# A two-layer encoder with a product-key expert stage: the next layer's inputs loaded in thirteen pieces beside thirteen tiles of the second table

## What is computed

```python
q = (xt @ w_query).reshape(T, PEER_HEADS, 2, PEER_DK // 2)
s = jnp.einsum('thpd,phkd->thpk', q, sub_keys)
s_top, i_top = lax.top_k(s, PEER_TOPK)
...
ue = jnp.take(u_tab, ib, axis=0)
a = jax.nn.gelu(jnp.einsum('thkd,td->thk', ue, xb), approximate=False)
ve = jnp.take(v_tab, ib, axis=0)
return jnp.einsum('thk,thkd->td', (gb * a).astype(ve.dtype), ve)
```

## Time and profile before

| | |
|---|---|
| median of three runs | 2057.51 us (2055.43 to 2057.92) |
| profiled execution, its own time | 2052.14 us |
| its span in the trace | 2050.3 us |
| PE busy in the span | 1958.4 us (96%) |
| granted clock of TensorE, mean | 0.988 of full speed |
| PE's share of the chain that ended last | 88% |
| DMA's share of that chain | 1% |
| second table's stage, layer 0 and layer 1 | 664 to 1023 us, 1680 to 2040 us |

### The profile page before, as it was taken

The page is one execution under the profiler, slowest core; times in us unless marked ns, Lnnn a source line. Parts: engine busy times, 40 slices in busy tenths (PEclk is TensorE's granted clock), DMA queues, the critical chain, the costliest instruction groups (busy, mean ns, idle before and its releaser), DMA issues.

```text
span 2050.3 us, 43061 instructions
## 1 busy us (share of the span) xinstructions
PE 1958.4 (96%) x12792; PEld 1786.3 (87%) x12792; DVE 1320.7 (64%) x2869; ACT 1103.0 (54%) x2124; POOL 770.4 (38%) x553
## 2 busy tenths in 40 slices
PE   7989998999999999999998999989999999999997
PEld 6779997999999887888777799979999998878886
DVE  4655699666666665666546557986666666656665
ACT  4344454666665554555533454546666555555554
POOL 4433599576770000000054316995777600000000
PEclk9999999999999999999999999999999999999999
DMA  5215454444344556555522154544343455565555
GB/s 209 74 42 174 153 178 144 153 143 140 137 142 173 187 194 235 192 194 194 185 73 82 55 182 150 179 145 151 134 143 135 141 178 191 194 244 194 194 190 179
DMA packets 90470, 327.05 MB, mean 160 GB/s; under 512 B 10400, under 2 KB 11168, under 8 KB 89760
## 3 DMA queue, kind: packets, MB, share of 16 engines
q1 hardware_dynamic: 90400, 326.18, 46.0%
HBM read 325.09 MB, written 1.05 MB: 159 GB/s over the span
## 4 chain that ended last, share of the span: by engine, by line
PE 88%; DVE 5%; issue 3%; POOL 2%; DMA 1%; ACT 1%; SPq 1%; DVEq 0%; POOLq 0%; ACTq 0%
PE ps L795 12%; PE ps L796 12%; PE ps L797 12%; PE ps L868 11%; PE ps L871 11%; PE ps L870 11%; PE ps L814 6%; PE ps L768 2%; PE ps L771 1%; PE ps L770 1%; POOL tab_lo L1239 1%; DVE work L1345 1%; DMA raw<-tab_v 1%; PE ps L579 1%; PE ps L545 1%
## 5 line engine op out<-in xcount | busy, mean ns | idle before, releaser
L1239 POOL TENSOR_TENSOR tab_lo<-raw,tab_hi 128x512 fp32r<-128x512 f32 x416 | 586.3, 1425 | 262.0 <-ACT tab_hi L1071 181.2
L795 PE MATMUL ps<-x_lo,tab_hi 128*128 128x256 f32 x2048 | 591.8, 289 | 22.1 <-POOL tab_lo L1239 18.9
L797 PE MATMUL ps<-x_hi,tab_lo 128*128 128x256 f32 x2048 | 579.1, 283 | 0.0
L796 PE MATMUL ps<-x_hi,tab_hi 128*128 128x256 f32 x2048 | 579.0, 283 | 0.0
L1652 DVE TENSOR_TENSOR tab_lo<-raw,tab_hi 128x512 fp32r<-128x512 f32 x512 | 354.2, 692 | 280.0 <-ACT tab_hi L1166 276.2
L1071 ACT ACTIVATE tab_hi<-raw 128x512 fp32r<-128x512 f32 x504 | 317.5, 631 | 338.9 <-PE ps L797 334.4
L795 PEld LDWEIGHTS ps<-x_lo,tab_hi 128*128 128x128 f32 x2048 | 392.0, 191 | 25.7 <-POOL tab_lo L1239 25.4
L868 PE MATMUL ps<-tab_lo,w_hi 128*128 128x512 f32 x1024 | 400.6, 391 | 7.5 <-DVE w_lo L1660 7.5
L870 PE MATMUL ps<-tab_hi,w_hi 128*128 128x512 f32 x1024 | 399.8, 390 | 0.0
L871 PE MATMUL ps<-tab_hi,w_lo 128*128 128x512 f32 x1024 | 399.8, 390 | 0.0
L796 PEld LDWEIGHTS ps<-x_hi,tab_hi 128*128 128x128 f32 x2048 | 392.5, 192 | 0.0
(11 more groups left out here) (204 smaller groups left out, 2527.5 us busy)
## 6 DMA issues: line engine op xcount, KB each, us to landing
raw<-tab_u SPq DMA_DIRECT2D x256, 512.0 KB, 3.2
raw<-tab_v SPq DMA_DIRECT2D x256, 512.0 KB, 3.2
raw<-w_proj SPq DMA_DIRECT2D x68, 512.0 KB, 3.5
raw<-w_proj SPq DMA_DIRECT2D x16, 384.0 KB, 3.1
work<-cdft SPq DMA_DIRECT2D x3, 1536.0 KB, 9.5
work<-cfilter SPq DMA_DIRECT2D x3, 768.0 KB, 5.4
work<-sub_keys SPq DMA_DIRECT2D x2, 1024.0 KB, 5.5
work<-pmat SPq DMA_DIRECT2D x3, 352.0 KB, 6.2
```

What stands on the lines that cost most here:

```text
L795: mm(bank, hi, x_lo[:, 4 * h + k, :], start=(h + k == 0), stop=False)
L796: mm(bank, hi, x_hi[:, 4 * h + k, :], start=False, stop=False)
L797: last = mm(bank, lo, x_hi[:, 4 * h + k, :], start=False, stop=(h + k == 4))
L1239: tt(half(tab_lo, s, h), half(raw, s, h), half(tab_hi, s, h).bitcast(F32), ALU.subtract).then_inc(lo_pool.sem, 1)
```

## The change

The eight DMAs between tiles 47 and 48 of the second table are gone. The same data is loaded in fifteen DMAs in thirteen steps, one step behind the issue of each of the tiles 36 to 48. Step 0 has the two filter inputs and `pvec`, steps 1 and 2 the rest of `pmat` in two pieces of 608 columns, steps 3 to 5 the rest of `cfilter` in three of 512, steps 6 to 11 `cdft` in six of 512, and step 12 `gain_qk`. The two waits on the split weights now stand behind the issue of tile 36. Tiles 36 to 51 are written out instead of looped. The start of the program makes its loads with the same helpers, so there too 5 DMAs become 12.

```diff
+PARAM_MATS, PARAM_PIECES, DFT_PIECES = 2, 5, 6
+FOLLOWING = 1 + PARAM_PIECES + DFT_PIECES + 1
...
-        params_in = sig("params_in", 48)
-        dft_in = sig("dft_in", 16)
+        params_in = sig("params_in", 16 * PARAM_PIECES)
+        dft_in = sig("dft_in", 16 * DFT_PIECES)
...
-            def load_params(layer):
-                sp.dma_start(fm[:, 192:704], pmat[layer, :, 192:704]).then_inc(params_in.sem, 16)
-                sp.dma_start(fc[:, 256:CF_N], cfilter[:, 256:CF_N]).then_inc(params_in.sem, 16)
-                sp.dma_start(fm[:, 704:1408], pmat[layer, :, 704:1408]).then_inc(params_in.sem, 16)
-
-            def load_late_params(layer):
-                sp.dma_start(dft, cdft[:, :]).then_inc(dft_in.sem, 16)
-                sp.dma_start(gqk, gain_qk[layer, :, :]).then_inc(gqk_in.sem, 16)
+            def load_params(layer, piece):
+
+                if piece < PARAM_MATS:
+                    a, b = 192 + 608 * piece, 192 + 608 * (piece + 1)
+                    sp.dma_start(fm[:, a:b], pmat[layer, :, a:b]).then_inc(params_in.sem, 16)
+                else:
+                    a, b = 256 + 512 * (piece - PARAM_MATS), 256 + 512 * (piece - PARAM_MATS + 1)
+                    sp.dma_start(fc[:, a:b], cfilter[:, a:b]).then_inc(params_in.sem, 16)
+
+            def load_late_params(layer, piece):
+                if piece < DFT_PIECES:
+                    a, b = 512 * piece, 512 * (piece + 1)
+                    sp.dma_start(dft[:, a:b], cdft[:, a:b]).then_inc(dft_in.sem, 16)
+                else:
+                    sp.dma_start(gqk, gain_qk[layer, :, :]).then_inc(gqk_in.sem, 16)
+
+            def load_following(layer, piece):
+
+                if piece == 0:
+                    load_filter_inputs(layer)
+                    sp.dma_start(pv[:, :], pvec[layer, :, :]).then_inc(pv_in.sem, 16)
+                elif piece <= PARAM_PIECES:
+                    load_params(layer, piece - 1)
+                else:
+                    load_late_params(layer, piece - 1 - PARAM_PIECES)
...
-                with sp.Fori(0, 12) as i:
+                with sp.Fori(0, 9) as i:
                     stream(i, tab_v, lo_dve, LO_V)
 
 
-                sp.wait_ge(*at(whi_done, l, LOADED_AHEAD // SEQ + 1))
-                sp.wait_ge(*at(wlo_done, l, LOADED_AHEAD // SEQ + 1))
-                load_filter_inputs(following)
-                load_params(following)
-                load_late_params(following)
-                sp.dma_start(pv[:, :], pvec[following, :, :]).then_inc(pv_in.sem, 16)
-                with sp.Fori(12, 32) as i:
+                for j in range(36, 52):
+                    load_tile(j, tab_v, lo_dve, LO_V)
+                    if j == 36:
+                        sp.wait_ge(*at(whi_done, l, LOADED_AHEAD // SEQ + 1))
+                        sp.wait_ge(*at(wlo_done, l, LOADED_AHEAD // SEQ + 1))
+                    if j - 36 < FOLLOWING:
+                        load_following(following, j - 36)
+                with sp.Fori(13, 32) as i:
                     stream(i, tab_v, lo_dve, LO_V)
...
-                pe.wait_ge(*at(params_in, l, 48))
+                pe.wait_ge(*at(params_in, l, 16 * PARAM_PIECES))
```

More of the change, by code:

```diff
@@ L377, in _ @@
             load_channels(0, 1)
-            load_params(0)
+            for piece in range(PARAM_PIECES):
+                load_params(0, piece)
             load_channels(0, 2)
             load_channels(0, 3)
-            load_late_params(0)
+            for piece in range(DFT_PIECES + 1):
+                load_late_params(0, piece)
             with sp.Fori(0, DEPTH) as l:
@@ L411, in _, with load_tile @@
                     sp.dma_start(raw[:, n, :], tab_u[l, n, :, :]).then_inc(raw_in[n].sem, 16)
+                def load_tile(j, table, signal, offset, s=None):
+                    slot = j % 4 if s is None else s
+                    sp.wait_ge(*at(signal, l, j * 2 + offset - 6))
+                    sp.dma_start(raw[:, slot, :], table[l, j, :, :]).then_inc(raw_in[slot].sem, 16)
                 def stream(i, table, signal, offset):
                     for s in range(4):
-                        j = i * 4 + s
-                        sp.wait_ge(*at(signal, l, j * 2 + offset - 6))
-                        sp.dma_start(raw[:, s, :], table[l, j, :, :]).then_inc(raw_in[s].sem, 16)
+                        load_tile(i * 4 + s, table, signal, offset, s)
                 with sp.Fori(1, EARLY // 4 + 1) as i:
@@ L449, in _ @@
             sp.wait_ge(mlp_in.sem, (DEPTH + 1) * 32)
-            sp.wait_ge(params_in.sem, (DEPTH + 1) * 48)
-            sp.wait_ge(dft_in.sem, (DEPTH + 1) * 16)
+            sp.wait_ge(params_in.sem, (DEPTH + 1) * 16 * PARAM_PIECES)
+            sp.wait_ge(dft_in.sem, (DEPTH + 1) * 16 * DFT_PIECES)
             sp.wait_ge(gqk_in.sem, (DEPTH + 1) * 16)
@@ L533, in _ @@
                 pe.wait_ge(*at(sumdif_done, l, 1))
-                pe.wait_ge(*at(dft_in, l, 16))
+                pe.wait_ge(*at(dft_in, l, 16 * DFT_PIECES))
                 for n, (m, c, src, bank) in enumerate((
@@ L1310, in _ @@
                 dve.wait_ge(*at(sine_done, l, 2))
-                dve.wait_ge(*at(params_in, l, 48))
+                dve.wait_ge(*at(params_in, l, 16 * PARAM_PIECES))
                 for b in range(TB):
```

## The result

The changed kernel took 2041.66 us (median of four runs, 2039.95 to 2044.49) against 2056.47 us for the kernel before (four runs, 2055.11 to 2057.92). The ratio is 0.9929, 95% interval 0.9912 to 0.9946: faster, by 0.5 to 0.9%. The profiled execution took 2039.95 us, span 2038.1.

The account below looks back on a forecast made before the run. PE was taken to bound the kernel. Stalls of 7.0 us and slow stretches of 4.2 us removed, nothing added, gave 11.2 us off the 2057.5 us median: 2046.3 us, range 2042.5 to 2052.5.

Parts of the forecast that it names:

- What bounds, and the cause: PE bounds, busy 96% of the span; it stops when second-table tile 48 is late behind eight loads.
- Its signs: Changed trace: no ACT wait for `tab_v`, PE step 0.227 us, clock 1.00, landings 3.2 to 5 us, DMA share about 0.9.
- stall and slow stretch: PE at tile 48, both layers: removing the stalls gains 7.0 us, the half-speed matmuls behind them 4.2, together 11.2.
- Late issue and late landing as two terms: Tile 48 is issued 3.12 us late and lands another 5.9 us late, in all 9.0 us.
- DMA work beside the tiles: Tiles 36 to 48: tile 1.5 us plus piece 1.0 us of the engines fits into 2.72 us; cost nothing.
- The upper bound: A piece takes as long as a tile, 1.5 us: PE would lose 1.1 us a layer, 2.2 together.
- SP, the landing of the inputs and the start: SP's added issues beside the tiles, inputs landing by tile 49, and seven more issues at the start: each taken as 0.
- B: Faster by less: slow stretch stays or a backlog costs 2.2 us; gain 7 to 9 us, 2048.5 to 2050.5 us; 14%.
- C: No difference: SP halts among the new issues beside the tiles, a smaller stall replaces the old; 2053.5 us; 10%.
- D: Slower: pieces and tiles don't fit the DMA engines; at 2.1 us a piece, 2062 us; 5%.
- E: Loads don't overlap: piece holds the queue 3.9 us, tile 3.2, 51 us a layer, about 2150 us; 1%.
- the last line of the sum: Gain of 11.2 us subtracted from the median of three runs, 2057.5 us, giving 2046.3 us.

Follow-up runs that it names:

- start_only: Kernel before with only the loads at the program's start made in pieces, the eight loads between tiles 47 and 48 kept: 2055.33 us, ratio 0.9998 to before.
- table_only: Changed kernel with the loads at the program's start whole again, pieces only beside the second table: 2042.50 us, ratio 0.9933 to the kernel before.
- busy_stall_16: Kernel before with 16 matmuls on constants put into PE's pause between tiles 47 and 48: 2051.95 us, ratio 0.9982 to the kernel before.
- pieces_in_row: Changed kernel with its fifteen loads all in a row between tiles 47 and 48: 2055.57 us, ratio 1.0003 to the kernel before.
- issue_only: Kernel before with the eight loads between tiles 47 and 48 cut to 8 columns each: 2042.31 us, ratio 0.9932 to the kernel before.
- double: Changed kernel plus one more 256 KB load beside each of tiles 37 to 48: 2041.11 us, ratio 0.9928 to the kernel before.
- quadruple: Changed kernel plus three more 256 KB loads beside each of tiles 37 to 48: 2068.89 us, ratio 1.0061 to the kernel before.
- c_before_2: Kernel before, unchanged, a single execution read for its trace: stalls and slow stretches cost 10.0 us in both layers together.

## Why the prediction was right about the place and wrong about the size

**What bounds, and the cause: right.** Its signs came: no wait of ACT for a tile, the step at 0.227 us and a clock of 1.00, landings of 3.2 to 4.2 us, a share of 0.87 at 290 GB/s. start_only and table_only show that the loads at the start count for nothing that the runs can tell.

**Removed, stall and slow stretch: right in kind, 11.2 us a little small.** busy_stall_16 separates the two and gives 3.1 us for the slow stretch (1.9 to 5.6) against 4.2. Four traces of the kernel before give 11.4 us for both together on average, and this is all that the traced executions differ by: their own times are 2053.5 us on average before (four) and 2042.1 after (three). The runs gave more: 66 runs of before in the five sessions have the median 2055.7, ten runs of the changed kernel 2043.0 (2039.95 to 2044.99), 12.7 us apart. The 1.3 us between that and 11.4 stay open; seven traces, with stalls that differ by up to 2.5 us among themselves, don't settle them.

**Late issue and late landing as two terms: misleading, without effect on the sum.** I wrote "In all 9.0 us late", made of 3.12 and 5.9. The arrival was late by that, but the two are not causes of their own: in pieces_in_row tile 48 arrives 0.2 us later although it is issued 3.0 us later, and issue_only has the late issue and no stall. The delay is the bytes in the queue.

**DMA work beside the tiles: right.** I took 1.0 us of the engines for a piece; 0.87 of the share over the stretch gives 0.87 x 2.72 - 1.5 = 0.9. The upper bound was too careful: at twice the load (double) nothing stops.

**SP, the landing of the inputs and the start: right at nothing.** The issue of tile 43 (773.79) was 0.3 us late, the largest effect beside the tiles; start_only is within the noise of before.

**The size rivals.** B did not come (the slow stretch was regained). C and D did not come; double was still free and quadruple, with four times the load beside the tiles, was not. E, in which a load holds the queue until it lands, did not come either. The Trainium skill, page "DMA: Bandwidth & Descriptors" (section "Bandwidth"), advises batches of 1 MiB or more; it measured loads issued by GpSimd, while SP issues these. Here the larger loads bought nothing: fifteen loads in a row cost the same as eight (ratio 1.0003), and two batches the same as thirteen steps.

**The failed step is the last line of the sum: the base, and beside it the size of the gain.** "I subtract the gain from the median: 2057.5 - 11.2 = 2046.3 us". The base was the median of three runs of a kernel whose runs go from 2051.3 to 2059.3 us; the median of all 66 is 2055.7, 1.8 us under it. The gain was 11.2 us where all runs give 12.7, 1.5 us more. The last 1.3 us of the 4.6 between forecast and result are luck of the draw: the first four runs of the changed kernel lay at 2041.66, all ten at 2043.0, which would have been inside the range.

The range let this happen. It allowed for a larger gain or for scatter, but not for both, and its lower end by its own working (2046.3 less 4 us) was 2042.3, not 2042.5. The same sum on the profiled execution's own time gave 2040.9, which the prediction names and then leaves outside its range. That this is nearer to the result is in part luck as well, since that execution was 3.6 us faster than the median of its kernel.

## What to carry to other kernels

When a bulk load shares a queue with a stream that feeds the bound engine, compare its backlog in time with the stream's spare (here 4.3 us until ACT waits, 5.5 until PE stops). Below that it cost nothing here, in whatever pieces; beyond it the stall cost a slow clock as well, about half as much again. It was enough to cut the batch so that each part stayed under the spare: two parts did as well as thirteen.

Where single runs of one kernel lie up to 8 us apart and the change is worth 13, three runs are a weak base. Make the sum on every base that there is (the profiled execution and the median), and let the range hold both.

## What the runs showed of the hardware

The slow stretch behind a pause comes in two sizes. Of twelve stretches seven cost 1.5 to 1.7 us and five 2.7 to 3.0 us, with nothing between, and the pause's length (3.4 to 4.6 us) does not set which. Nor does it always start with the first matmul, as the timeline of PE in start_only, layer 0, shows:

```profile
802.96 0.49 PE L876 MATMUL ps<-tab_lo,w_hi 128*128 128x512 f32 x1 [3.45 <-DVE w_lo L1668]
803.29 0.39 PE L878 MATMUL ps<-tab_hi,w_hi 128*128 128x512 f32 x1
803.52 0.40 PE L879 MATMUL ps<-tab_hi,w_lo 128*128 128x512 f32 x1
803.75 0.59 PE L876 MATMUL ps<-tab_lo,w_hi 128*128 128x512 f32 x1
804.14 0.63 PE L878 MATMUL ps<-tab_hi,w_hi 128*128 128x512 f32 x1
```

After the pause three matmuls still run at the full rate (behind a filled pause, too, the first step is 0.32 us), and only then does the level fall. Three of the twelve stretches begin so. The Trainium skill, page "TensorE: Matmul & The Clock Gate" (part 1), says that the same kernel shows different numbers of slow matmuls at its start from run to run. Behind these pauses it is the same: in layer 0 of the kernel before, 13 steps were slow in the first trace and 7 in c_before_2 (2.8 and 1.5 us).

The scatter of the traced executions has two sources: the stalls with their slow stretches (10.0 to 12.5 us in the kernel before) and the mixing stages (422.0 to 426.2 us). In the windows 33 to 160 us and 1023 to 1230 us the granted clock was 0.94 to 0.99, where it was 1.00 in the first table's stage (160 to 664 us). That the clock sets the length of the mixing stages is likely and not shown.
